# Five reorderings in a hybrid decoder kernel: transposes between matmul groups, the state hops' bank and order, two sums of squares and two low halves

## What is computed

```python
# even layer: HGRN2 heads and RWKV-7 heads side by side
h = rmsnorm(x, norm_g)
z = h @ w_in                       # all branches and the gates in one projection
oa = hgrn2(...)                    # 8 heads of 128
ob = rwkv7(...)                    # 16 heads of 64, a state from token to token
x = x + (concat(oa, ob) * silu(gate)) @ w_out
x = x + (p[0] @ ple_proj[0]) * sigmoid(rmsnorm(x, ple_norm[0]) @ ple_gate[0])
# odd layer: block-sparse attention and a linear recurrence (RG-LRU)
x = x + (concat(moba(...), rglru(...)) * silu(gate)) @ w_out
x = x + (p[1] @ ple_proj[1]) * sigmoid(rmsnorm(x, ple_norm[1]) @ ple_gate[1])
return rmsnorm(x, final_norm)
```

## Time and profile before

| | us |
|---|---|
| median of 3 runs | 1198.02 (1192.04 to 1199.78) |
| the profiled execution, its own time | 1196.96 |
| its span, first to last instruction | 1195.2 |
| mean granted TensorE clock | 0.995 |
| PE busy | 1153.8 (97% of the span) |
| PEld busy | 910.6 (76%) |
| DVE busy | 760.9 (64%) |
| POOL busy | 629.2 (53%) |
| ACT busy | 446.5 (37%) |

### The profile page before, as it was taken

The page is one execution under the profiler, slowest core; times in us unless marked ns, Lnnn a source line. Parts: engine busy times, 40 slices in busy tenths (PEclk is TensorE's granted clock), DMA queues, the critical chain, the costliest instruction groups (busy, mean ns, idle before and its releaser), DMA issues.

```text
span 1195.2 us, 31036 instructions
## 1 busy us (share of the span) xinstructions
PE 1153.8 (97%) x12076; PEld 910.6 (76%) x12076; DVE 760.9 (64%) x1339; ACT 446.5 (37%) x844; POOL 629.2 (53%) x594
## 2 busy tenths in 40 slices
PE   7899999999999999999999999998999999999996
PEld 5678777777788788777887878786777777777874
DVE  7874684675666746855666441648458686967637
ACT  5452343333523433434335310325234444352224
POOL 5552452442444524434344667866557475749862
PEclk9999999999999999999999999999999999999999
DMA  5221121211111211212212143323223232323331
GB/s 197 80 64 47 54 73 30 65 54 44 60 54 55 66 46 54 65 38 65 55 46 71 48 150 115 97 88 88 79 64 88 71 88 61 92 58 97 97 88 70
DMA packets 46890, 87.38 MB, mean 73 GB/s; under 512 B 5824, under 2 KB 7104, under 8 KB 46656
## 3 DMA queue, kind: packets, MB, share of 16 engines
q1 hardware_dynamic: 44496, 81.04, 22.9%
q10 hardware_dynamic: 2288, 4.72, 1.1%
HBM read 83.65 MB, written 2.10 MB: 72 GB/s over the span
## 4 chain that ended last, share of the span: by engine, by line
PE 75%; DVE 14%; ACT 3%; issue 3%; DVEq 0%; ACTq 0%
PE psum L394 72%; ACT mix L1160 2%; DVE mix L1718 2%; DVE mix L2383 1%; DVE mix L2361 1%; PE psum L1064 1%; DVE mix L2370 1%; DVE mix L2381 1%; PE psum L546 1%; DVE h_split L1722 1%; ACT L1160 0%; DVE mix L1740 0%; DVE mix L2469 0%; DVE psum L1838 0%; DVE mix L2010 0%
## 5 line engine op out<-in xcount | busy, mean ns | idle before, releaser
L394 PE MATMUL psum<-h_split,w_hi 128*128 128x512 f32 x2320 | 752.1, 405 | 17.5 <-DVE h_split L1718 8.0
L394 PEld LDWEIGHTS psum<-h_split,w_hi 128*128 128x128 f32 x2320 | 423.0, 189 | 124.2 <-issue 31.1
L348 POOL TENSOR_SCALAR w_hi<-w_raw 128x512 fp32r<-128x512 f32 x290 | 208.8, 720 | 505.7 <-PE psum L394 359.4
L394 PE MATMUL psum<-h_split,w_lo 128*128 128x512 f32 x1160 | 455.6, 393 | 0.6 <-issue 0.6
L350 POOL TENSOR_TENSOR w_lo<-w_raw,w_hi 128x512 fp32r<-128x512 f32 x290 | 408.4, 1408 | 24.2
L394 PEld LDWEIGHTS psum<-mix 64*64 64x64 f32 (+3 forms) x8256 | 231.1, 138 | 75.8 <-issue 52.5
L1160 ACT ACTIVATE mix<-psum 128x512 f32<-128x512 f32 (+4 forms) x292 | 140.8, 496 | 392.6 <-PE psum L394 244.6
L394 PE MATMUL psum<-mix 64*64 64x64 f32 (+5 forms) x8256 | 273.5, 236 | 8.6 <-ACT mix L1160 2.3
L394 PEld LDWEIGHTS psum<-h_split,w_lo 128*128 128x128 f32 x1160 | 219.0, 189 | 48.4 <-issue 0.3
L1160 ACT ACTIVATE mix<-mix 128x512 f32<-128x512 f32 (+3 forms) x256 | 131.4, 547 | 120.3 <-DVE mix L2253 49.1
L1838 DVE COPY_PREDICATED mix<-mask,psum 128x128 f32<-128x128 uint8 (+1 forms) x192 | 82.8, 469 | 38.9 <-PE psum L394 36.4
(11 more groups left out here) (136 smaller groups left out, 672.1 us busy)
## 6 DMA issues: line engine op xcount, KB each, us to landing
w_raw<-wall SPq DMA_DIRECT2D x290, 256.0 KB, 2.6
mix<-xT SPq DMA_DIRECT2D x4, 512.0 KB, 7.2
mix<-xT ACTq DMA_DIRECT2D x1, 2048.0 KB, 8.0
out<-mix SPq DMA_DIRECT2D x7, 256.0 KB, 2.6
mix<-pT ACTq DMA_DIRECT2D x2, 512.0 KB, 3.7
mix<-lru_w ACTq DMA_DIRECT2D x4, 256.0 KB, 3.2
mix<-w2a ACTq DMA_DIRECT2D x16, 32.0 KB, 2.2
mask<-mask_u SPq DMA_DIRECT2D x1, 432.0 KB, 6.5
```

The lines of the kernel that those rows point to most:

```text
L348: pool.tensor_scalar(w_hi[:, slot, :, :], w_raw[:, slot, :], 1.0, 0.0, ALU.mult, ALU.add).then_inc(sem["w_hi"], 1)
L394: return pe.matmul(o, lhsT, rhs, start=start, stop=stop, skip_group_check=True)
```

## The change

Five edits of order. None adds or removes an instruction of an engine; one wait is moved and one destination changes.

1. Transposes (`even_round`, rounds 1 to 7): at levels 2 and 3 the four transposes of `token_rows` stand between the P and the N groups, where `value_rows` stands at level 4. `last_round` keeps its order.
2. Hop 1 writes bank 5 (`H1`) instead of bank 7, and does not wait for `rw_rp`; hop 2 waits for it. DVE reads hop 1 from there.
3. DVE: the second half of level 3 stands behind `hop_state(r, 4)` and `hop_add(r, 5)`, not ahead of them.
4. `gate_projection`, both uses: `sumsq` stands behind tile 6 of c = 0, and tile 7 of c = 0 behind tile 2 of c = 1.
5. The low halves 4 and 5 are made between the two blocks of the last recurrence.

```diff
-                    pe.wait_ge(sem["rw_rp"], count("rw_rp", r))
                 else:
                     pe.wait_ge(sem["rw_s"], count("rw_s", r, c - 2))
-                mm(R1[:, 0:64], m_t[:, c, :], state(c)).then_inc(sem["rw_c"], 1)
+                    if c == 2:
+                        pe.wait_ge(sem["rw_rp"], count("rw_rp", r))
+                mm(hop_bank(c), m_t[:, c, :], state(c)).then_inc(sem["rw_c"], 1)
...
                         if lvl == 4:
                             value_rows(r)
+                        else:
+                            token_rows(r, lvl, True)
                         inverse_n(r, lvl, 0)
                         inverse_n(r, lvl, 1)
-                        if lvl < 4:
-                            token_rows(r, lvl, True)
                         t(3, 2 * lvl - 2, 2 * lvl)
...
+                for n in range(7):
+                    product(0, n)
+                sumsq(stage, bank[0])
+                pe.wait_ge(sem["h_ready"], count("h_ready", stage, 1))
+                for n in range(3):
+                    product(1, n)
+                product(0, 7)
+                for n in range(3, KC):
+                    product(1, n)
...
                     hop_add(r, 4)
-                    between(level, 3, (1,))
                     hop_state(r, 4)
                     hop_add(r, 5)
+                    between(level, 3, (1,))
                     hop_state(r, 5)
...
                     if b == 0:
                         lru_output(r, 0)
+                        for c in between:
+                            odd_output_low(c)
...
-            lru_states(OD_ROUNDS - 1)
+            lru_states(OD_ROUNDS - 1, (4, 5))
             lru_output(OD_ROUNDS - 1, 1)
-            for c in range(4, 4 + KC):
+            for c in range(6, 4 + KC):
```

More of the change, by code:

```diff
@@ L258, in state, with hop_bank @@
             return n_add[:, 0, :] if c == 1 else s_all[:, c, :]
+        def hop_bank(c):
+            return (H1 if c == 1 else R1)[:, 0:64]
         def by_parity(ap):
@@ L989, in gate_projection, with product @@
             def gate_projection(stage, unit0):
-                for c in range(4):
-                    pe.wait_ge(sem["h_ready"], count("h_ready", stage, c))
[L993 to L1006, removed]
+                def product(c, n):
+                    u = unit0 + 2 * c + n // 4
+                    if n % 4 == 0 or c == 1 and n == 3 or c == 0 and n == 7:
+                        pe.wait_ge(sem["w_ready"], count("w_ready", u))
+                    if c == 0 and n < 7:
+                        pe.wait_ge(sem["x_added"], count("x_added", stage - 1, n + 1))
+                    elif c == 0:
+                        pe.wait_ge(sem["ln_done"], count("ln_done", stage))
+                    last = split_products(bank[(n + 1) % 8], u % SLOTS, n % 4, h_split[:, c, :], h_split[:, KC + c, :], c == 0, False)
+                    if n % 4 == 3:
+                        last.then_inc(sem["units_done"], 1)
@@ new lines, in gate_projection @@
+                pe.wait_ge(sem["h_ready"], count("h_ready", stage, 0))
+                for n in range(7):
[7 more added lines that the diff above has]
+                    product(1, n)
+                for c in (2, 3):
+                    pe.wait_ge(sem["h_ready"], count("h_ready", stage, c))
+                    for n in range(KC):
+                        product(c, n)
@@ L2029, in hop_state @@
                 dve.wait_ge(sem["rw_c"], count("rw_c", r, c - 1))
-                stt(s_all[:, c + 1, :], R1[:, 0:64], e_pos[:, c, RL:RL + 1], s_next, ALU.mult, ALU.add).then_inc(sem["rw_s"], 1)
+                stt(s_all[:, c + 1, :], hop_bank(c), e_pos[:, c, RL:RL + 1], s_next, ALU.mult, ALU.add).then_inc(sem["rw_s"], 1)
             def pair_norm(r):
@@ L2375, in lru_output, with lru_states @@
                 dve.tensor_tensor(row(4 + b, r, 2), u_th[b], og[:, 1 + b, :], ALU.mult).then_inc(sem["ru_y"], 1)
-            def lru_states(r):
+            def lru_states(r, between=()):
                 for b in range(2):
```

## The result

| | before | after |
|---|---|---|
| median of 9 runs, us | 1197.46 | 1186.46 |
| profiled execution: span, us | 1195.2 | 1184.1 |
| mean granted TensorE clock | 0.995 | 0.996 |

The ratio is 0.9914, 95% interval 0.9897 to 0.9932: 0.86% faster, 10.3 us, with an interval of 8.1 to 12.3 us. 1187.0 was predicted. One of the nine runs before was a slow one, 1286.74 us, and the ratio leaves it out.

What follows compares the result with a forecast made beforehand. PE, busy for 97% of the span, was taken as the bound, so reordering wins only its short stalls: 2.2 + 2.8 + 2.1 + 1.9 + 2.0 = 11.0 us, median 1187.0 us (0.92% less), range 1181.5 to 1193.5.

Steps and rivals of the forecast that it cites:

- Edit 1: Levels 2 and 3 of seven rounds: transposes between P and N hide a wait, 14 x 0.16 = 2.2 us won.
- Edit 2: Hop 1 no longer waits for DVE's readers: 7 x 0.40 = 2.8 us won; hop 2 fits by 0.1 us.
- Edit 3: Hop 5 no longer waits for `hop_state` 4 on DVE: 7 x 0.30 = 2.1 us won, margin less than 0.1.
- Edit 4: Gate projections: both sums of squares stop waiting for DVE's last addition, 2 x 0.97 = 1.9 us won.
- edit 5: Odd output projection, fifth block: the stall for the low halves goes, the whole 2.0 us won.
- Gains in the rounds are not given back at their end.: Rounds: work of DVE, ACT and POOL starts on PE's results and moves with it, so gains stay.
- If PE's unexplained pauses became more: Sign that the prediction is wrong: more PE pauses without explanation than the 2.3 us in three places.
- The clock: Whole span: clock granted at 0.995 of full speed (2.4 GHz) throughout, and the same expected after the change.
- A: Hops 2, 5 and 6: DVE takes PE's place, about half of edits 2 and 3 lost, 1189.5 us; chance 0.17.
- B: Levels 2 and 3: turns of the array nearly free, 3.4 us more won, 1183.6 us; chance 0.11.
- C: 28 added array turns drain longer: slower from 0.51 us a turn, 1211.6 us at 1.0; chance 0.03.
- D: Hop 1 waits for transition matrices, or hop 5 for the hop before: 4.9 us less won, 1191.9; chance 0.09.

Runs made afterwards that it cites:

- the repetition: The kernel after, unchanged, measured once more on the same chip: 1186.73 us, ratio 0.9911 to the kernel before.
- the kernel with the keys later: Kernel after, with the product of HGRN2's keys (`hg_keys`) one step of the projection later: 1185.52 us, ratio 0.9908 to before.
- The kernel of the thresholds: Kernel after, sums of squares only one and two products later than in before, only low half 4 moved: 1187.59 us (1 run).
- the bank alone: Kernel before, with hop 1 writing bank 5 but still waiting for DVE's readers: 1196.29 us, ratio 1.0001 to before.

## Why the prediction held, step by step

- **Edit 1, 14 x 0.16 = 2.2 us.** 14 x 0.14 = 2.0 by the starts, 1.9 by the kernel with edit 1 alone. The sizes inside it were off: the turn to full size was taken at 0.13 and is 0.14, the turn back was taken at under 0.1 and is 0.16. The allowance that transposes behind tiles may be spaced wider (0.19 cut to 0.16) covered most of it. The wait that went is then 0.14 + 0.31 = 0.45 us a level. The point from which edit 1 by itself loses is thus 0.22 us a turn, 0.06 above what was measured: the margin of this edit is thin, and a level with one more turn would have almost none. The Trainium skill, "TensorEngine Tiling (Array Packing)", Key Properties, says that a change of tiling mode drains TensorE. The runs agree that a turn costs time, 0.14 and 0.16 us; whether that time is a drain, starts alone don't show.
- **Edit 2, 7 x 0.40 = 2.8.** Held: the gap is 0.23 in each of the seven rounds, and 2.6 us by the kernel with edit 2 alone. Hop 2 is not held instead, and its margin of 0.1 was there. The way to it was off by little: it comes 0.92 us behind hop 1, not 1.0.
- **Edit 3, 7 x 0.30 = 2.1.** 0.28 to 0.29, held in the trace. Alone it showed 1.2 us by the ratio, which its interval doesn't tell from 2.0. The margin of "less than 0.1" at hop 5 was enough in all seven rounds (gap 0.15).
- **Edit 4, 1.9, and edit 5, 2.0.** Held to 0.1 (1.94 and 2.03), and 4.4 together by the ratio. Tile 7 had 1.2 us of margin, 0.7 predicted.
- **The sum, 11.0 us.** 10.8 by the starts, 10.3 and 10.7 by the ratios of the two measurements of the whole, whose intervals reach from 8 to 12 us. The ratios of the four kernels with parts of the change add to 0.85%, the whole is 0.86%, but each has an interval of 0.12 to 0.18% to either side. They don't exclude the 2 to 3 us that the profiles of the whole lose again in the rounds. Edit 2 alone hands 0.03 us a round to hop 5, and with edit 3 there even that is gone.
- **"Gains in the rounds are not given back at their end."** Not at their end, but inside them: 4.1 us of 6.8 are left in the profiles. The prediction put this at nothing, as it followed only the waits on DVE, ACT and POOL.
- **"If PE's unexplained pauses became more".** They did, as the prediction had named for a sign that it was wrong: by the list of waits 2.3 us became 4.0, and 5.7 in the repetition. The profiled execution came out at the sum all the same, since a stretch at the lower clock, 1.4 us, was absent. Each edit's own term is thus shown at its place; that the total agreed within 0.7 us is in part luck.
- **The clock.** It was not "0.995 throughout". That is a mean, and before has two stretches of 3.41 us at 1.2 GHz. One of them costs 1.4 us.
- **DVE's share of the chain** was said to lie mostly in the gate stages and in the tail. Of its 168 us 75 lie between 860 and 1080 us, in the odd layer's rounds, 34 between 770 and 860 and 30 behind 1080. No term used this.

**Rivals.** A (DVE takes PE's place at hops 2, 5 and 6) falls: no wait there in any round after. B (turns nearly free, 3.4 us more) falls by the measured turns. C (turns of 0.51 us and up) falls too: they are at under a third of that. D (edits 2 and 3 don't do what they say) falls by the three kernels of those edits.

## What to carry over

Where PE is busy for 97% and stands still for some tenths of a microsecond in many places, read the starts of neighbouring matmuls rather than the idle times, and add up each stall with the margin of what is late next; here that gave 11.0 us from the trace of before alone, where the starts show 10.8. Then ask what else PE will run into when it comes sooner: here its own instructions, which no list of waits on other engines shows, and a comparison of one profile with one other hid it. Work of another tile size put into a wait costs the turns of the array between tile sizes: 0.45 us of waiting here bought 0.31 of turns, so count them and price each from a row. Terms of 1 to 2 us are at the edge of what ten timed runs that span 5 us can tell, so judge each by its gap in the trace, and the sum by the time.

## What was not expected of the hardware

**The lower clock comes and goes.** At the start of the odd layer PE stands still again and again for DVE's `h_split` (by starts 1.3 and 2.1 us, and some 8 us on 0.9 in before and 1.2 in after, and 1.7 in both). Behind these waits the granted clock falls to 1.2 GHz for 3.41 us: twice in before, once in after and in its repetition, and not at all in the kernel with the keys later, whose instructions there are those of after. Of the six profiles without edits 1 to 3 together four have two such stretches there and two have one; of the six with them one has two. The kernel of the thresholds shows one stretch of 10.24 us. Its window, and that of the kernel with the keys later:

```profile
830.00:840.00 10.00, 9.27 (x20) 6.13 (x21) 6.93 (x11) 3.85 (x6) 3.69 (x4) 0.52 0.20 52
```

```profile
830.00:840.00 10.00, 7.38 (x28) 5.05 (x29) 8.10 (x11) 3.89 (x6) 4.42 (x4) 1.00 0.19 52
```

The falls stand behind a time in which PE did little: the kernels with edit 1 alone and with the bank alone have one at 1089, behind the stall at block 4, and the one with edit 3 alone has the one at 280.6. Why the same stall is followed by a fall in one execution and by none in another isn't settled. Where PE has work, a fall costs 1.4 to 1.6 us: 1.4 at the second place, and 1.6 at 1089, the time by which the two kernels that have it there take longer than before from there to the end. The stall at block 4 goes with edit 5: of the five profiles without edit 5 two have a fall behind it, of the seven with it none has. That would be a gain beside the 2.0 us of the stall, but five and seven profiles are too few to show it.

**PE waits for its own instructions.** The pauses that the waits list as "issue" have a cause that the traces hold and the list doesn't name. The page of the profile lists a DMA queue of kind "instruction" in every profile, here that of before (queue, kind: packets, MB, share):

```profile
q8 instruction: 91, 1.49, 0.5%
```

These are 91 packets of 16 KB. They come 4 us apart where PE runs tiles of 64x64 and some 29 us apart in the gate stages, in the median every 250 of PE's matmuls and weight loads, so they are PE's program. Places in four profiles (us; the last column is from the landing of the packet to PE's next matmul):

| profile | packet | lands at | PE's starts around the pause | landing to start |
|---|---|---|---|---|
| before | 28th | 279.79 | 279.49 and 281.09 | 1.30 |
| after | 28th | 277.86 | 277.48 and 279.35 | 1.49 |
| before | 57th | 521.76 | 522.19 and 523.16 | 1.39 |
| after | 57th | 517.83 | 517.93 and 519.16 | 1.33 |
| edit 1 alone | 28th | 276.95 | no pause (279.04) | 2.09 |
| edits 4 and 5 | 28th | 277.02 | no pause (279.67) | 2.65 |

The twelve profiles (before, after and ten experiments) have 43 such pauses of over 0.25 us idle. Each of them ends 1.24 to 1.58 us behind the landing of one of these packets, and at one place it is always the packet of the same number: the 28th between 276 and 282 us in ten profiles, the 57th between 515 and 524 in all twelve. Where the packet landed earlier against PE's progress, as in the last two rows, there is no pause. So PE stands for its own instructions.

The pauses also go with the edits. The "issue" waits of the six profiles that have edits 1 to 3 together add up to 3.4 to 5.7 us, those of the six others to 0.8 to 2.6. The means are 2.4 us apart, where the rounds lose 2.7 of their 6.8. At 417 to 421 us the first six all have a pause, with starts 0.5 to 1.0 us apart; of the others edit 2 alone has 0.4 there and the rest 0.2. Two things can be behind it, and no run parts them: with these edits PE comes to a packet's first instruction sooner, and with edit 2 the packet is wanted earlier in the program. In all seven profiles with edit 2 PE resumes two matmuls earlier at the 57th packet than in the five without, and one earlier at the 28th. All this is read from traces: no run changed when the packets come, and what sets their time stays open.
